# Two products of the second mixer taken on the residual, with the norm's root multiplied in behind them

## The reference

```python
x = x + g2 * conv_ffn(h2, w_up[l], conv_w[l], conv_b[l], w_down[l], rows)
...
return rmsnorm(x, norm_final)        # end of the first block
...
h = rmsnorm_2(x, g_mix)              # start of the second
proj = h @ w_in
...
dn_qkv = jax.nn.silu(causal_dwconv(dn_qkv, dn_conv_w))   # 4 taps over the tokens
dq, dk_, dv_ = [...]
```

## Time and profile before

| | us |
|---|---|
| median of 3 runs | 974.74 (973.21 to 975.86) |
| the profiled execution | 974.95 |
| its span | 973.2 |

### The profile page before, as it was taken

How to read it: one execution, slowest core, us unless ns; L and a number is a source line. 1 busy time by engine, 2 the same in 40 slices (tenths; PEclk the granted TensorE clock), 3 DMA queues, 4 the chain that set the end, 5 groups by cost and what they waited for, 6 DMA issues and landing times.

```text
span 973.2 us, 17918 instructions
## 1 busy us (share of the span) xinstructions
PE 946.9 (97%) x7656; PEld 891.1 (92%) x7656; DVE 718.3 (74%) x1036; ACT 490.3 (50%) x610; POOL 14.9 (2%) x34
## 2 busy tenths in 40 slices
PE   6999999999989999999999999999999999999997
PEld 4689999999989999989999899999999999999986
DVE  3689988888898988857966885545676776666663
ACT  3544435635545565438754743324644645444563
POOL 0000000002000000000200000000000000000000
PEclk9999999999999999989999999999999999999999
DMA  9998354465548656424563334433365455655541
GB/s 339 348 289 263 114 174 131 131 216 159 175 148 274 227 182 213 170 87 157 201 207 132 127 118 154 132 131 114 104 191 177 170 177 182 208 173 185 186 150 44
DMA packets 114046, 171.77 MB, mean 177 GB/s; under 512 B 3240, under 2 KB 96704, under 8 KB 109872
## 3 DMA queue, kind: packets, MB, share of 16 engines
q1 hardware_dynamic: 111680, 165.63, 50.8%
q0 software_dynamic: 1088, 2.57, 0.9%
q10 hardware_dynamic: 1200, 2.43, 0.7%
HBM read 169.55 MB, written 1.06 MB: 175 GB/s over the span
## 4 chain that ended last, share of the span: by engine, by line
PE 65%; DVE 8%; ACT 4%; issue 2%; DVEq 0%; ACTq 0%
PE bank L1164 20%; PE bank L1165 19%; PE bank L1166 19%; DVE wlo L622 3%; PE bank L1731 2%; DVE arena L2234 1%; ACT whi L613 1%; PE bank L1198 1%; ACT arena L973 1%; DVE arena L2320 1%; DVE arena L1911 1%; PE bank L1203 0%; DVE arena L1901 0%; PE bank L1490 0%; DVE XT L2186 0%
## 5 line engine op out<-in xcount | busy, mean ns | idle before, releaser
L1164 PE MATMUL bank<-hhi,whi 128*128 128x256 f32 (+1 forms) x1744 | 506.5, 290 | 7.3 <-issue 1.6
L1165 PE MATMUL bank<-hlo,whi 128*128 128x256 f32 (+1 forms) x1744 | 500.2, 287 | 0.0
L1166 PE MATMUL bank<-hhi,wlo 128*128 128x256 f32 (+1 forms) x1744 | 500.1, 287 | 0.0
L622 DVE TENSOR_TENSOR wlo<-raw,whi 128x2048 fp32r<-128x2048 f32 x131 | 299.7, 2289 | 118.0 <-ACT whi L613 90.7
L1164 PEld LDWEIGHTS bank<-hhi,whi 128*128 128x128 f32 x1744 | 334.2, 192 | 15.2 <-issue 10.0
L1165 PEld LDWEIGHTS bank<-hlo,whi 128*128 128x128 f32 x1744 | 334.3, 192 | 4.0 <-issue 1.2
L1166 PEld LDWEIGHTS bank<-hhi,wlo 128*128 128x128 f32 x1744 | 334.2, 192 | 2.5
L613 ACT ACTIVATE whi<-raw 128x2048 fp32r<-128x2048 f32 x131 | 250.1, 1913 | 82.5 <-PE bank L1166 68.9
L1164 PE MATMUL bank<-whi,hhi 128*128 128x256 f32 (+1 forms) x256 | 87.6, 342 | 0.8 <-ACT arena L1124 0.8
L1165 PE MATMUL bank<-wlo,hhi 128*128 128x256 f32 (+1 forms) x256 | 86.5, 338 | 0.0
L1166 PE MATMUL bank<-whi,hlo 128*128 128x256 f32 (+1 forms) x256 | 86.4, 337 | 0.0
(11 more groups left out here) (353 smaller groups left out, 843.0 us busy)
## 6 DMA issues: line engine op xcount, KB each, us to landing
raw<-in_w_up_dram SPq DMA_DIRECT2D x44, 1024.0 KB, 5.2
raw<-in_w_in_tiles_dram SPq DMA_DIRECT2D x32, 1024.0 KB, 4.9
raw<-in_w_down_dram SPq DMA_DIRECT2D x22, 1024.0 KB, 4.8
raw<-in_w_ada_dram SPq DMA_DIRECT2D x19, 1024.0 KB, 5.3
raw<-in_w_in_dram SPq DMA_DIRECT2D x14, 1024.0 KB, 5.5
raw<-in_w_branch_dram SPq DMA_DIRECT2D x6, 1024.0 KB, 5.0
arena<-in_w_ada_dram SPq DMA_DIRECT2D x10, 512.0 KB, 9.5
raw<-in_w_out_dram SPq DMA_DIRECT2D x4, 1024.0 KB, 5.1
```

Source lines behind the costliest of these rows:

```text
L622: dve.tensor_tensor(wlo[:, g % RING, :], raw[:, n % RING, :], whi[:, g % RING, :].bitcast(F32), ALU.subtract).then_inc(w_lo, 1)
L1164: pe.matmul(o, wh, ah, start=start, stop=False, **kw)
L1165: pe.matmul(o, wh, al, start=False, stop=False, **kw)
L1166: return pe.matmul(o, wl, ah, start=False, stop=stop, **kw)
```

## The change

`dq0` and `dq1` are no longer computed from the normalised `HT2` but from `XT` times `gain2`, which needs no root. The parts of this plain product lie in columns of `hhi` and `hlo` that are free then (`P_AT`). ScalarE writes the high part behind each square (two copies with a scale for each pair of k), VectorE the low part one pair behind its residuals (`plain_low`). TensorE runs `dq0` straight behind `down(10)`, with the last two `both_sums` before k = 6, then `dq1` one half at a time, with the spreading of the two roots between the halves; all keep_clock matmuls of this place are gone. VectorE copies the spread root out of its bank (`roots`) and multiplies each of the two products by it on the way into `dq_n` (`roots_out`), which empties the banks; `conv_start` and `conv_dn` of `dq0` and `dq1` read `dq_n`. `dk0` is now the first product on `HT2`, `sm` stands behind it, and the third group of `norm_hi` waits for `dq1`, whose parts lie where it writes. The splits that were called behind the normalising (`adv("fd9")`, the weights of `dq1`, and `adv("fd10")`, those of `dk0`) now stand ahead of it on both engines.

```diff
@@ scalar @@
-            squares(lambda c: (x_new, c + 1))
...
+            adv("fd9")
+            act.wait_ge(weigh_ready, 2)
+            for c in range(4):
+                act.wait_ge(x_new, c + 1)
+                act.activation(SQ[:, 512 * c:512 * (c + 1)].rearrange("p (k t) -> p k t", k=2),
+                               XT[:, 2 * c:2 * c + 2, 0:T], ACT.Square).then_inc(sq_ready, 1)
+                for k in (2 * c, 2 * c + 1):
+                    ins = act.activation(hhi[:, P_AT[k]:P_AT[k] + T], XT[:, k, 0:T], ACT.Copy, scale=gain2[:, k:k + 1])
+                ins.then_inc(plain_hi, 1)
+            adv("fd10")
...
-            adv("fd9")
-            norm_hi(HT2, 6)
+            norm_hi(HT2, 6, held=lambda g: (g_full, g_no("dq1") + 1) if g == 2 else None)
...
-            adv("fd10")
@@ tensor @@
-            both_sums(2)
-            both_sums(3).then_inc(m_full, 1)
-            keep_clock(bank[4], 5)
...
-            keep_clock(bank[4], 5)
...
+            def parts_and_sums(k, nb):
+
+                if nb == 0 and k % 2 == 0:
+                    if k == 6:
+                        both_sums(2)
+                        both_sums(3).then_inc(m_full, 1)
+                    pe.wait_ge(plain_hi, k // 2 + 1)
+                    pe.wait_ge(plain_lo, k // 2 + 1)
...
+            product_plain("dq0", [(k, nb) for k in range(KT) for nb in range(2)], parts_and_sums)
+            product_plain("dq1", [(k, nb) for nb in range(2) for k in range(KT)], spread_roots)
...
-            gemm_first("dq0", T, 12)
+            gemm_first("dk0", T, 12)
...
-            gemm("dq1", T)
-            gemm("dk0", T)
@@ vector @@
+            def plain_low(c):
+
+                dve.wait_ge(plain_hi, c + 1)
+                for k in (2 * c, 2 * c + 1):
+                    s_ = slice(P_AT[k], P_AT[k] + T)
+                    ins = dve.scalar_tensor_tensor(out=hlo[:, s_], in0=XT[:, k, 0:T], scalar=gain2[:, k:k + 1],
+                                                   in1=hhi[:, s_].bitcast(F32), op0=ALU.mult, op1=ALU.subtract)
+                ins.then_inc(plain_lo, 1)
...
+            plain_low(3)
+            adv("fd9")
...
+            adv("fd10")
             dve.wait_ge(m_full, m_no("sum3") + 1)
+            link(dve.tensor_copy(roots, m_bank("sum3")[:, 0:T]))
+
+            def roots_out(n):
+
+                dve.tensor_tensor(dq_n[n], two(g_wait(f"dq{n}")), roots.unsqueeze(1).broadcast_to([P, 2, T]), ALU.mult
+                                  ).then_inc(g_empty["dve"], 1)
+            roots_out(0)
...
             low_parts(HT2, T, None, 12, 3)
-            adv("fd9")
-            adv("fd10")
+            roots_out(1)
```

More of the change, by code:

```diff
@@ L345, in build @@
         HT2 = slot(4, 2)
+        P_AT = [3072 + T * k for k in range(4)] + [T * k for k in range(4, 8)]
+        roots = slot(11, 1, 0, T)
+        dq_n = [slot(7, 1, 512 * n, 512).rearrange("p (j t) -> p j t", j=2) for n in range(2)]
         QC, KC, VC, KB, QD = h4(0), h4(1), h4(2), h4(3), h4(5)
@@ L649, in norm_std, with norm_hi @@
                                ).then_inc(m_empty["act"], 1)
-            def norm_hi(ht, f0, steps=(1, 2, 3, 4), shift=None):
+            def norm_hi(ht, f0, steps=(1, 2, 3, 4), shift=None, held=None):
                 w = ht.shape[1] // KT
@@ L655, in norm_hi @@
                     act.wait_ge(*(g_done(f"xt{2 * g + 1}") if f0 is None else (h_f32, f0 + steps[g])))
+                    if held is not None and held(g):
+                        act.wait_ge(*held(g))
                     if shift is not None:
@@ L893, in conv_start @@
             def conv_start(u, dst, tap):
-                g_wait(u)
+                if u[:2] == "dq":
+                    act.wait_ge(*g_done(u))
+                    src = dq_n[int(u[2])]
+                else:
+                    g_wait(u)
+                    src = two(g_bank(u))
                 for t in range(2):
-                    ins = act.activation(dst[:, t, :], g_bank(u)[:, T * t:T * (t + 1)], ACT.Copy,
-                                         scale=par("dn_conv", k=36 + tap + t))
+                    ins = act.activation(dst[:, t, :], src[:, t, :], ACT.Copy, scale=par("dn_conv", k=36 + tap + t))
                 ins.then_inc(acc_start, 1)
@@ L1537, in _, with product_plain, spread_roots @@
             down(FFT // 2 - 1)
-            both_sums(2)
-            both_sums(3).then_inc(m_full, 1)
-            keep_clock(bank[4], 5)
[L1541 to L1544, removed]
-            keep_clock(bank[4], 5)
+            def product_plain(name, order, at):
+                wh, wl = w_parts(name, KT)
+                o = g_open(name)
+                for k, nb in order:
+                    at(k, nb)
+                    ws = [x[:, k, P * nb:P * (nb + 1)] for x in (wh, wl)]
+                    a = [h[:, P_AT[k]:P_AT[k] + T] for h in (hhi, hlo)]
+                    ins = product(o[:, T * nb:T * (nb + 1)], ws, a, k == 0 and (nb == 0 or order[1] != (0, 1)),
+                                  k == KT - 1, skip_group_check=True)
+                ins.then_inc(g_full, 1)
+            def parts_and_sums(k, nb):
[5 more added lines that the diff above has]
+                    pe.wait_ge(plain_lo, k // 2 + 1)
+            def spread_roots(k, nb):
+                if (k, nb) == (0, 1):
+                    for n, u in enumerate(("sum3", "norm1")):
+                        o = m_open(u)
+                        pe.wait_ge(diag_ready, n + 1)
+                        pe.matmul(o[:, 0:T], ones, diag[:, T * n:T * (n + 1)], start=True, stop=True
+                                  ).then_inc(m_full, 1)
+            product_plain("dq0", [(k, nb) for k in range(KT) for nb in range(2)], parts_and_sums)
+            product_plain("dq1", [(k, nb) for nb in range(2) for k in range(KT)], spread_roots)
             def l_open(u):
@@ L2307, in _ @@
             low_parts(HT2, T, None, 12, 3)
-            adv("fd9")
-            adv("fd10")
+            roots_out(1)
             def conv_dn(u, dst, tap):
                 dve.wait_ge(acc_start, dn_no[u] + 1)
-                ps = g_wait(u)
+                if u[:2] == "dq":
+                    src, done = dq_n[int(u[2])], conv_q
+                else:
+                    src, done = two(g_wait(u)), g_empty["dve"]
                 last = [None, None]
@@ L2320, in conv_dn @@
                         ins = dve.scalar_tensor_tensor(
-                            out=dst[:, t, d:T], in0=ps[:, T * t:T * (t + 1) - d],
+                            out=dst[:, t, d:T], in0=src[:, t, 0:T - d],
                             scalar=par("dn_conv", k=12 * (3 - d) + tap + t), in1=dst[:, t, d:T], op0=ALU.mult,
@@ L2325, in conv_dn @@
                             last[t] = mark(ins)
-                ins.then_inc(g_empty["dve"], 1)
+                ins.then_inc(done, 1)
                 adv(u)
```

11 lines of the change are left out of this document (7 added, 4 removed).

## The result

The changed kernel takes 977.05 us (median of 11 runs, 975.50 to 984.28) beside 974.74 us for the kernel before on the same chip (11 runs). The ratio is **1.0044, 95% interval 1.0024 to 1.0064**: slower by 4.3 us (2.3 to 6.2). A second, later comparison gave 1.0047 (1.0028 to 1.0066).

A forecast was written before the change was run, and what follows sets the result against it. The prediction took VectorE and ScalarE, waiting for the root, to bound the kernel ahead of `dv0`. A `dv0` 1.2 us later plus 2.2 us at half rate made 3.4 us more, 978.1 us; range 975.4 to 979.9.

The forecast's parts named there:

- What bounds: Before `dv0`, VectorE and ScalarE alone set the time for 30 us; what counts is when they get the root.
- Rival 3: Whole kernel: TensorE was the bound after all and its head start survives, up to 7.4 us less, 967.3 us; chance 0.08.
- TensorE up to S: From the last `down` at 425.34 to the vector engines getting the root, forecast at 436.3 us; nothing starves.
- rival 2: Inside `dq0`, at the side-by-side `both_sums`: the clock falls already there, root 1.7 us later, 979.8 us; chance 0.08.
- S 2.1 us later: The vector engines get the spread root at 436.3 us instead of 434.23, 2.1 us later.
- Copy and multiply: On VectorE after the root: copying `roots` and multiplying for `dq0` add 1.0 us (0.8 to 1.3).
- The convolution of `dq0`: On VectorE, waiting for ScalarE to start the accumulator: begins at 445.45 us, 1.1 us later than before.
- `dv0` 1.2 us later: At `dv0`, after the shifted block on VectorE and ScalarE: start at 465.45 us, 1.2 us later.
- The half rate: At the start of `dv0`, after idle time: half rate for 3.4 to 5.6 us, costing 2.2 us (outside 1.3 to 3.4).
- Rival 1: At `dv0`: the rate stays up or returns at once, leaving only 1.2 us more, 975.9 us; chance 0.12.
- the clock's term: At the start of `dv0`: 2.2 us lost to half rate after TensorE's idle gap.
- the root's term: From the root, coming 2.1 us later, through the vector engines' work: `dv0` starts 1.2 us later.

The follow-up runs named there:

- the first trace: Unchanged kernel before, the traced execution the prediction rests on: normalising 8.69 us behind the last residual, k sums 50.30 us; kernel's median 974.74 us.
- the three with the early root: Unchanged kernel before, its second, third and fourth traces: normalising 7.14 us behind the last residual, k sums 48.76 us.
- the filled gap: Kernel after plus 20 unread keep_clock matmuls in TensorE's idle time, 15 ahead of the transpose and 5 behind it; ratio 1.0034 (1.0016 to 1.0051).
- the second trace of after: Kernel after, unchanged, traced and timed again: `dv0` 40.09 us and k sums 54.24 us behind the last residual; ratio 1.0047.

## Why the prediction was right, and the step that was wrong

The forecast was 978.1 us, 3.4 more; measured were 977.05 us and 4.3 more. By its steps, after's times with 2.02 added:

- **What bounds.** Right. A root moved later in the kernel before reached the time in full, one moved earlier only until TensorE's own products decided, and the head start of the plain products brought nothing while the vector engines were as late. Rival 3 is out: TensorE stood idle from 454.3 (456.3; forecast 455.8) to 463.6.
- **TensorE up to S.** 10.96 us from the end of the last `down` forecast, 11.06 measured (423.32 to 434.38). VectorE's split ended 0.36 us ahead of the root; 0.4 was forecast. Nothing starved, and the two `both_sums` side by side left the clock at 1.00, so rival 2 is out.
- **S 2.1 us later.** Right beside the first trace (2.17), wrong beside the three with the early root (3.7). This is the step that does not hold in general: "the keep_clock matmuls that they replace cost about the same". It priced them from one execution in which all of them ran at half rate. I had the 6.8 us of low rate in front of me with a single 3.4 us elsewhere, and took its place and length as fixed. The "3.4 us of products" in the same sentence is a slip as well: by the terms listed above it, k 6 and 7 and the first half of `dq1` are 1.5 + 2.9 = 4.4 us. The sum does not use it.
- **Copy and multiply.** 1.0 forecast, 1.06 measured.
- **The convolution of `dq0`.** 445.45 forecast (its terms add to 445.41), 445.59 measured; the splits that moved away bought nothing because ScalarE was last, as forecast, with 1.72 us of wait.
- **`dv0` 1.2 us later.** 1.37 measured. The two convolutions from plain memory take 2.45 us beside 2.42.
- **The half rate.** The mechanism is shown by the filled gap; the size was 2.2 forecast and 2.7 measured (2.6 in the second trace of after). The products run 6.1 us at 1.2 GHz (5.8 in the second), above the 3.4 to 5.6 of the estimate and inside its outer bound. Rival 1 is out. The rule of the Trainium skill, page "TensorE: Matmul & The Clock Gate", section "HAM oscillation — how this bites in real kernels", that a burst after idle time starts throttled, held here: the products of `dv0` lay 0.21 us apart from their start.

The sum of the terms beside the first trace is 4.1 us where 3.4 were forecast, and 5.6 beside the traces with the early root. That the timed difference, 4.3, came out close to 3.4 is partly luck: the clock's term was 0.5 too small, and against an execution with the early root the root's term is too small by 1.55 as well. The chances hung on the low rate lasting over 3.4 us; it lasted 6.1.

## What to carry to other kernels

Work given to TensorE early is worth only as much as the engine that releases its next bank is early too: follow the chain from the new products to the first instruction that someone waits for, and move that engine's order with them. Idle time won on TensorE is not neutral, since it can cost the clock for the burst behind it; 20 matmuls without a user in the gap took back 2.7 us by the traces. Before pricing matmuls at half rate from one trace, look at a second one of the same kernel: whether they ran at half rate can differ between executions of the same program, 1.55 us here.

## What the runs showed of the hardware

- In four traces of one unchanged kernel the clock fell at the same place in the program each time, but at 1.9 us behind the last residual in one and about 3.1 us in the others, and stayed low for 6.8 us in the one and 3.4 in the others. Two further kernels with the same instructions up to there fell at 1.8 and 2.2 us and stayed low for 6.8. With the long idle time of the kernel after it was low for 10.2 us in both traces (459.5 to 469.7 in the first), with two waits of 2 us for 3.4.
- Sixteen matmuls of two columns on end (from 427.64 in the kernel after) between dense products did not bring the clock down, in any of six traces of the kernel after and its variants; eight of them with 0.94 us of idle time ahead, at the same place in the kernel before, went with a fall in all seven traces of it and its variants.
- A multiply-add on VectorE is no faster when neither operand comes from a bank: 2.45 us for six beside 2.42.
